# First block of a three-layer transformer: keys, values and indexer first as plain fp32, heads beside convolution projections, modulation in quarter slabs

## The chip, the cores and the metric

The kernel runs on one core of a Trainium2 chip. The core has TensorE (PE; weight loads are PEld), VectorE (DVE), ScalarE (ACT), GpSimd (POOL) and SyncE (SP), whose only work here is to issue DMAs in a queue of its own. The metric is device time in microseconds (us) of one execution, as a median of runs.

## The reference

One token mixer with a sparse indexer, modulated by a vector `c`, then a gated linear attention layer and a differential attention layer, all with feed-forwards, on 256 tokens of width 1024, batch 1, in fp32. The change lies in the first block:

```python
mod = c_act @ w_ada[l] + b_ada[l]                     # 1024 x 6144
sh1, sc1, g1, sh2, sc2, g2 = jnp.split(mod, 6, axis=-1)
mix = token_mixer(modulate(x, sh1, sc1), w_in[l], ...)
x = layer_norm(ALPHA * x + g1[:, None, :] * mix, ln1_g[l], ln1_b[l])
ff = swiglu(modulate(x, sh2, sc2), w_gate[l], w_up[l], w_down[l])
x = layer_norm(ALPHA * x + g2[:, None, :] * ff, ln2_g[l], ln2_b[l])
...
def token_mixer(h, w_in, conv_w, attn_norm_g, conv_norm_g, w_out, cos, sin):
    q, k, v, qi, ki, wi, gate_b, gate_c, hc = jnp.split(h @ w_in, offsets, axis=-1)
    # q (8 heads of 64), k (one head), qi (8 x 32) and ki get a partial rope
    # rel = relu(qi . ki); score = sum over heads of rel * wi; causal
    # each query keeps its 64 best keys; softmax attention of 8 heads over them
    attn = group_rms_norm(attn, attn_norm_g, N_HEADS_ATTN)
    u = gate_c * hc
    conv = sum(conv_w[j] * u_pad[:, j:j + s, :] for j in range(CONV_K))
    conv_out = group_rms_norm(gate_b * conv, conv_norm_g, CONV_GROUPS)
    return jnp.concatenate([attn, conv_out], axis=-1) @ w_out
```

## The kernel before

Activations lie transposed, features on the 128 partitions, as eight tiles of 128 x 256. Weights stream through two 2 MB buffers `raw` in SBUF (slots 0 and 1), 512 columns of a matrix at a time (a slab, 128 x 8 x 512). A product in near-fp32 is three fp32r matmuls: ScalarE rounds a slab into `whi` (`split`, L811), VectorE takes the rest into `wlo` (`low`, L1165), each in quarters of 1024 columns, and TensorE adds hi·hi, lo·hi and hi·lo (L1739 to L1741). A tile of output is 8 x 3 matmuls of 256 columns. The table of `Phase` objects (`plan`) fixes the order of the slabs, their slots and who must have read a buffer before it may be loaded again.

SyncE walks that table and waits, in order, for each buffer's reader. All engines run straight-line code, so what stands first on an engine runs first, and who waits holds up everything behind it.

The first block: slabs 0 to 3 of `w_ada` (shift and scale) are multiplied by `c` on VectorE, eight chunks of 512 columns (`modulate`, L1216 to L1221), and summed over partitions by TensorE (`modulation`, L1846, four matmuls with one column). GpSimd makes the modulated input `om` (L620), ScalarE its rounded form `ohi` (L883), VectorE `olo` (L1246). Then come the slabs `in_q`, `in_idx` (indexer queries, keys in copies), `in_v` (values and indexer weights), `in_gc`, the index scores, `in_hc` with the short convolution, the top-k on VectorE (L1325 to L1335), `in_gb`, and then the loop over eight heads. A head is: scores (PE L1927), masked logits and maxima (DVE L1360, L1363), exponentials (ACT L950), division (DVE L1371, L1374), transposes (PE L1943), `prob_t` (ACT L962), values (PE L1953). The modulation slabs 4, 5, 6, 7 and 11 go over ScalarE (`scale_by_c`, L924: eight chunks times `c`) and GpSimd (`sum_slab`, L631 to L635: three halving sums), and GpSimd issues their loads itself; slabs 8, 9 and 10 go over VectorE inside the head loop. All twelve are done ahead of `out0`, the output projection (two slabs, eight tiles), beside which TensorE sums the means and squares of layer norm 0 (L1968, L1970) one tile behind the residual addition (DVE L1405). Behind it: layer norm, `gate_up0`, `down0`, and the two other layers.

## Time and profile before

| what | us |
|---|---|
| median of 3 runs | 1215.05 (1214.82 to 1218.31) |
| the profiled execution | 1212.0 |
| its span | 1210.2 |
| TensorE busy | 1095.4 |
| VectorE busy | 753.9 |
| ScalarE busy | 585.8 |
| GpSimd busy | 258.9 |

Matmuls overlap, so a busy TensorE is not one at its peak: what counts is the distance between the starts of two matmuls and the granted clock (1.00 is 2.4 GHz, 0.50 is 1.2 GHz). The slabs are moved at up to some 400 GB/s, with a mean of 160 over the span.

### The profile page before, as it was taken

To read this page: it belongs to the slowest core of one execution; us is meant where nothing else is said; L and a number is where in the kernel's file an instruction comes from. 1 tells how busy PE (TensorE), PEld (TensorE's weight loads), DVE (VectorE), ACT (ScalarE), POOL (GpSimd) and SP (SyncE) were. 2 spreads that over 40 slices of the span, in tenths; PEclk is the share of its full clock that TensorE was granted. 3 is DMA by queue.
4 is the path that set the end of the run, shared out by engine and by line. 5 is a ranking of instruction groups with operands and counts; after the bars stand their busy time and mean duration, and the time that the engine had idled before them with its cause. 6 is when DMAs were issued, how large, how long until landed. Compare 5 with 4: busy or idle time off the path is not lost.

```text
span 1210.2 us, 20957 instructions
## 1 busy us (share of the span) xinstructions
PE 1095.4 (91%) x8179; PEld 1011.6 (84%) x8179; DVE 753.9 (62%) x1164; ACT 585.8 (48%) x989; POOL 258.9 (21%) x253
## 2 busy tenths in 40 slices
PE   1899638989999998999999999998997899999998
PEld 1887524879999996888899999997885599999997
DVE  5747876656655446775665664566777676655554
ACT  0545334574554338551564444465555664544452
POOL 0434332003332002101133331022120023332001
PEclk9988855999999999998999999998999999999999
DMA  8754454426554625350265455573432045554650
GB/s 317 219 209 164 184 189 159 144 81 219 184 186 126 206 79 207 141 210 1 70 209 184 169 160 157 169 273 112 162 116 100 1 166 204 186 186 123 200 186 36
DMA packets 188325, 193.46 MB, mean 160 GB/s; under 512 B 13721, under 2 KB 150722, under 8 KB 188130
## 3 DMA queue, kind: packets, MB, share of 16 engines
q1 hardware_dynamic: 184016, 179.88, 44.2%
q0 software_dynamic: 2640, 10.49, 2.3%
q10 hardware_dynamic: 1602, 2.18, 0.5%
q8 instruction: 45, 0.74, 0.2%
q14 instruction: 22, 0.18, 0.0%
HBM read 191.48 MB, written 1.05 MB: 159 GB/s over the span
## 4 chain that ended last, share of the span: by engine, by line
PE 65%; DVE 18%; ACT 6%; DMA 5%; issue 4%; POOL 1%; ACTq 1%; POOLq 0%; SPq 0%; DVEq 0%
PE gemm L1739 19%; PE gemm L1740 19%; PE gemm L1741 19%; DVE wlo L1165 5%; DVE macc L1218 2%; ACT whi L811 2%; DMA raw<-in_w_in 2%; PE aux L2062 1%; POOL om L620 1%; DVE xlo L1187 1%; PE aux L1846 1%; ACT om L984 1%; DMA early<-in_w_ada 1%; DMA raw<-in_w_ada 1%; ACT ohi L982 1%
## 5 line engine op out<-in xcount | busy, mean ns | idle before, releaser
L1165 DVE TENSOR_TENSOR wlo<-raw,whi 128x1024 fp32r<-128x1024 f32 (+2 forms) x348 | 399.6, 1195 | 137.3 <-ACT whi L811 137.0
L1739 PE MATMUL gemm<-ohi,whi 128*128 128x256 f32 x1536 | 436.7, 284 | 18.4 <-DVE wlo L1165 8.4
L1741 PE MATMUL gemm<-ohi,wlo 128*128 128x256 f32 x1536 | 431.4, 281 | 0.0
L1740 PE MATMUL gemm<-olo,whi 128*128 128x256 f32 x1536 | 431.1, 281 | 0.0
L811 ACT ACTIVATE whi<-raw 128x1024 fp32r<-128x1024 f32 (+2 forms) x348 | 309.5, 955 | 75.4 <-PE gemm L1741 52.2
L1739 PEld LDWEIGHTS gemm<-ohi,whi 128*128 128x128 f32 x1536 | 291.5, 190 | 28.9 <-DVE wlo L1165 11.9
L1740 PEld LDWEIGHTS gemm<-olo,whi 128*128 128x128 f32 x1536 | 291.6, 190 | 0.2
L1741 PEld LDWEIGHTS gemm<-ohi,wlo 128*128 128x128 f32 x1536 | 291.2, 190 | 0.0
L1739 PE MATMUL gemm<-acthi,whi 128*128 128x256 f32 x528 | 147.7, 280 | 0.0
L1740 PE MATMUL gemm<-actlo,whi 128*128 128x256 f32 x528 | 147.4, 279 | 0.0
L1741 PE MATMUL gemm<-acthi,wlo 128*128 128x256 f32 x528 | 147.3, 279 | 0.0
L664 POOL TENSOR_TENSOR prod<-sg,ut 128x256 f32<-128x256 f32 x66 | 48.7, 739 | 311.2 <-DVE ut L1492 163.8
L1739 PEld LDWEIGHTS gemm<-acthi,whi 128*128 128x128 f32 x528 | 99.1, 188 | 0.2
L1740 PEld LDWEIGHTS gemm<-actlo,whi 128*128 128x128 f32 x528 | 99.1, 188 | 0.0
L1741 PEld LDWEIGHTS gemm<-acthi,wlo 128*128 128x128 f32 x528 | 99.0, 188 | 0.0
L1010 ACT ACTIVATE sg<-gt 128x256 f32<-128x256 f32 x66 | 27.6, 418 | 133.2 <-DVE gt L1492 89.4
L668 POOL TENSOR_TENSOR actlo<-prod,acthi 128x256 f32 (+1 forms) x63 | 74.5, 1183 | 0.0
L1740 PE MATMUL gemm<-xlo,whi 128*128 128x256 f32 x256 | 72.3, 282 | 0.0
L1740 PEld LDWEIGHTS gemm<-xlo,whi 128*128 128x128 f32 x256 | 49.0, 191 | 1.4 <-issue 1.4
L701 POOL TENSOR_TENSOR sq_sum<-sq_sum,dsq 128x256 f32<-128x256 f32 x28 | 21.0, 748 | 129.6 <-ACT dsq L830 129.6
L1492 DVE TENSOR_TENSOR ut<-gemm,rstd 128x256 f32<-128x256 f32 x44 | 18.4, 419 | 48.2 <-PE gemm L1741 48.2
L1739 PE MATMUL gemm<-dhi,whi 128*128 128x256 f32 x128 | 39.8, 311 | 4.7 <-DVE xlo L1187 4.6
(315 smaller groups left out, 1508.6 us busy)
## 6 DMA issues: line engine op xcount, KB each, us to landing
raw<-in_ffn_w_in SPq DMA_DIRECT2D x44, 1024.0 KB, 6.3
raw<-in_ffn_w_out SPq DMA_DIRECT2D x32, 704.0 KB, 5.7
raw<-in_gla_w_in SPq DMA_DIRECT2D x6, 2048.0 KB, 7.8
raw<-in_diff_w_in SPq DMA_DIRECT2D x6, 2048.0 KB, 7.7
raw<-in_w_gate SPq DMA_DIRECT2D x11, 1024.0 KB, 5.1
raw<-in_w_up SPq DMA_DIRECT2D x11, 1024.0 KB, 7.3
raw<-in_w_down SPq DMA_DIRECT2D x16, 704.0 KB, 5.0
raw<-in_w_ada SPq DMA_DIRECT2D x5, 2048.0 KB, 8.3
```

The costliest lines, as they stand in the source:

```text
L620: me.did(pool.tensor_scalar(tl(om, t), tl(res, t), mod[:, 8 + t:9 + t], mod[:, t:t + 1], ALU.mult, ALU.add), om_ready)
L664: pool.tensor_tensor(tl(prod, j), tl(sg, j), tl(ut, j), ALU.mult).then_inc(prod_done, 1)
L668: pool.tensor_tensor(tl(actlo, t - 1), tl(prod, 1 - j), tl(acthi, t - 1).bitcast(F32), ALU.subtract).then_inc(actlo_ready, 1)
L701: pool.tensor_tensor(sq_sum[:, :], sq_sum[:, :], src, ALU.add).then_inc(squares_summed if last else sq_added, 1)
L811: act.activation(whi[hslot][:, q * w:(q + 1) * w], raw[slot][:, q * w:(q + 1) * w], ACT.Copy).then_inc(hi_ready, 1)
L1010: act.activation(tl(sg, j), tl(gt, j), ACT.Silu).then_inc(silu_done, 1)
L1165: dve.tensor_tensor(wlo[hslot][:, q * w:(q + 1) * w], raw[slot][:, q * w:(q + 1) * w], whi[hslot][:, q * w:(q + 1) * w].bitcast(F32), ALU. ...
L1218: me.link(dve.scalar_tensor_tensor(acc, src[:, 512 * k:512 * (k + 1)], c_act[:, k:k + 1], acc, ALU.mult, ALU.add))
L1492: ins = dve.tensor_tensor(dst, bank[:, 0:T], rstd[:, 0:T], ALU.mult)
L1739: pe.matmul(dst, st_hi, mv_hi, start=start, stop=False)
L1740: pe.matmul(dst, st_hi, mv_lo, start=False, stop=False)
L1741: return pe.matmul(dst, st_lo, mv_hi, start=False, stop=stop_)
```

## The change

- `in_idx` and `in_v` are gone. Their columns are one slab `in_kv` of 424 columns without copies, and TensorE multiplies them as plain fp32 with `om` (four banks, 8 x 4 matmuls of 256 columns), ahead of `in_q`. Keys and indexer keys are rotated once and copied to the other partitions by ScalarE; values are transposed.
- The index scores stand between the tiles of `in_q`; the top-k follows on VectorE, beside `in_gc`.
- The head loop has one tile of `in_hc` (heads 0 to 3) or `in_gb` (heads 4 to 7) in each head, with their convolution and gating steps. `in_gb` is split at heads 0 and 1, `out0` at heads 4 and 5.
- `om` and `ohi` both come from ScalarE. For slabs 0 to 3 VectorE takes six chunks and TensorE the last two; SyncE no longer waits for the parameter rows.
- Slabs 4, 5 and 6 keep the way over ScalarE and GpSimd, but their loads are in SyncE's queue; slab 6 is scaled and summed behind the head loop. Slabs 7 to 11 come in quarters (two chunks, 0.5 MB, two small buffers) and are taken by VectorE (`modulate_part`): slab 7 early, 8 and 9 one quarter beside each tile of `out0`, 10 and 11 one beside each slab of `gate_up0`.
- The transposes of `p` move from the first block into `down0`.

```diff
-    ada = lambda i: Phase(f"ada{i}", 1, SLAB, 0, 1, by="pool" if i in POOL_SLABS else "dve",
-                          ahead=False, ring=i not in (2, 3), slot=0 if i in (0, 8, 9, 11) else 1)
+    ada = lambda i: Phase(f"ada{i}", 1, SLAB, 0, 1, by="pool" if i in POOL_SLABS else "mod", ahead=False,
+                          ring=i not in (2, 3), slot=0 if i == 0 else 1)
+    mixer = lambda name, slot: Phase(name, 1, SLAB, 4, 1, ahead=False, slot=slot)
     phases = [
         ada(0), ada(1), ada(2), ada(3),
-        Phase("in_q", 1, SLAB, 4, 1, slot=0), Phase("in_idx", 1, SLAB, 4, 7, slot=1),
-        Phase("in_v", 1, 8 * 72, 2, 2, slot=0), ada(4), Phase("in_gc", 1, SLAB, 4, 1, slot=0), ada(5),
-        Phase("in_hc", 1, SLAB, 4, 1, slot=0), ada(6), Phase("in_gb", 1, SLAB, 4, 1, ahead=False, slot=0), ada(7),
-        ada(8), ada(9), ada(10), ada(11),
-        Phase("out0", 2, SLAB, 4, 1, slot=1), *ffn(0),
+        Phase("in_kv", 1, 8 * KV, 0, 1, by="kv", ahead=False, slot=0), mixer("in_q", 1), mixer("in_gc", 0), ada(4),
+        mixer("in_hc", 0), ada(5), mixer("in_gb", 0), ada(6),
+        Phase("out0", 2, SLAB, 4, 1, slot=0), *ffn(0),
...
+            def load_part(n):
+                wait(sp, part_used, n - 1)
+                dst, src = ada_part(n)
+                sp.dma_start(dst, src).then_inc(part_in[n % 2], 16)
...
+            parts = lambda *ns: [lambda n=n: load_part(n) for n in ns]
+            behind = {("ada1", 0): [load_x], ("in_q", 0): [*parts(0, 1), load_const, *parts(2, 3)],
+                      ("ada6", 0): parts(4, 5), ("gate_up0", 0): parts(6, 7), ("gate_up0", 1): parts(8, 9, 10, 11),
+                      ("gate_up0", 2): parts(12, 13), **{("gate_up0", i): parts(10 + i) for i in range(4, 10)},
...
-                if ph.by == "pool":
...
-                    if i == 0:
-                        sp.wait_ge(params_in, 16 * (len(ROWS_A) + len(ROWS_B) + 4))
...
+            for buf, ready in ((om, om_ready), (ohi, ohi_ready)):
+                for t in range(KT):
+                    me.did(act.activation(tl(buf, t), tl(res, t), ACT.Identity, bias=mod[:, t:t + 1],
+                                          scale=mod[:, 8 + t:9 + t]), ready)
...
+            def beside_head(i):
+                if i in (0, 1):
+                    split_all("in_gb", "in_gc", range(2 * i, 2 * i + 2))
+                if i == 2:
+                    scale_by_c(5)
+                if i in (4, 5):
+                    split_all("out0", "in_hc", range(2 * i - 8, 2 * i - 6))
+                if i == 6:
+                    group_squares(0, attn_ready, 2)
+                if i == 7:
+                    group_root(0, G[0])
+                    group_squares(2, gated_ready, 2)
+            exponentials(0)
+            for i in range(NH):
...
+            group_squares(1, attn_ready, 4)
...
+            prep(order=(4, 5))
+            group_root(3, X[0])
+            prep(order=(6, 7))
+            group_root(1, X[1])
+            prep(order=(2, 3))
             scale_by_c(6)
-            gemm("in_gb")
-            group_root((2, 3), mixed, mix_sq, 1.0 / HD, 0, X[0:2])
...
+            def modulate_part(n):
+                i, part_ = PART_SLABS[n // PARTS], n % PARTS
+                acc = MOD_SUM[i][:, :]
+                dve.wait_ge(part_in[n % 2], 16 * (n // 2 + 1))
+                if part_ == 0:
+                    wait(dve, mod_done, sum_free(i))
+                for j in range(2):
+                    k = 2 * part_ + j
+                    w, c = part[n % 2][:, 512 * j:512 * (j + 1)], c_act[:, k:k + 1]
+                    if k == 0:
+                        me.link(dve.tensor_scalar(acc, w, c, None, ALU.mult))
+                    else:
+                        me.link(dve.scalar_tensor_tensor(acc, w, c, acc, ALU.mult, ALU.add),
+                                part_used if j else None)
...
-            me.did(dve.tensor_tensor(fold[:, 32:40], A("ln2_g", 0, 8), B("norm_mix_2", 0, 8), ALU.mult))
-            me.link(dve.tensor_tensor(fold[:, 40:48], A("ln2_b", 0, 8), B("norm_mix_2", 0, 8), ALU.mult))
-            for q in range(4):
-                low(PH["out0"], At(0), q)
-            me.again(mixed_ready)
-            prep(mix_make, order=(0, 1, 2, 3))
+            masked_maxima(0)
+            for i in range(NH):
+                probabilities(i)
+                if i + 1 < NH:
+                    masked_maxima(i + 1)
+                for q in {1: (0, 1), 2: (2, 3)}.get(i, ()):
+                    low(PH["in_gb"], At(0), q)
+                for q in {5: (0, 1), 6: (2, 3)}.get(i, ()):
+                    low(PH["out0"], At(0), q)
+                if i < 4:
+                    short_conv(i)
+                else:
+                    gated_conv(i - 4)
+                if i in (2, 4, 6):
+                    take_pair(i // 2 - 1)
+            me.again(attn_ready)
+            prep(mix_make, order=(0, 1), free=PH["in_gb"].tile0 + 4)
+            take_pair(3)
+            me.again(gated_ready)
+            prep(mix_make, order=(4, 5))
+            prep(mix_make, order=(6, 7))
+            me.again(attn_ready)
+            prep(mix_make, order=(2, 3))
+            dve.wait_ge(mod_done, 7)
...
-            add_to_residual("out0", 16)
+            add_to_residual("out0", 16, lambda at, t: modulate_part(PARTS + 4 * at.i + t))
...
+                def part_beside(at, t):
+                    if t == 3 and 1 <= at.i <= 2 * PARTS:
+                        modulate_part(3 * PARTS + at.i - 1)
...
-                pe.wait_ge(pool_summed if i in POOL_SLABS else dve_summed, ph.used0 + 1)
+                if i < 4:
+                    src = raw[PH[f"ada{i}"].slot] if i < 2 else early[i - 2]
+                    pe.wait_ge(landed[i] if i < 2 else early_in[i - 2][1], 16)
+                    for k in (KT - 2, KT - 1):
+                        for m in range(4):
+                            pe.matmul(X[3][:, 4 * i + m:4 * i + m + 1], src[:, 512 * k + P * m:512 * k + P * (m + 1)],
+                                      c_act[:, k:k + 1], start=k == KT - 2 and m == 0, stop=False, skip_group_check=True)
+                    pe.wait_ge(dve_summed, i + 1)
+                elif i in POOL_SLABS:
+                    pe.wait_ge(pool_summed, POOL_SLABS.index(i) + 1)
...
+            modulation(2)
             modulation(3)
-            keep_warm(G[2], 13, ones[:, :])
+            keep_warm(G[2], 4, ones[:, :])
+            ph = PH["in_kv"]
+            w = flat(ph.slot, KT, KV)
+            pe.wait_ge(landed[ph.slot], ph.landed[0])
+            for k in range(KT):
+                pe.wait_ge(om_ready, k + 1)
+                for bank, (c0, c1) in zip(G, (K_V, KI_WI, QI_A, QI_B)):
+                    if k == 0:
+                        banks.claim(bank, rope_src)
+                    ins = pe.matmul(bank[0:c1 - c0, 0:T], w[:, k, c0:c1], tl(om, k), start=k == 0, stop=k == KT - 1)
+                    if k == KT - 1:
+                        ins.then_inc(kv_done, 1)
...
-                    h = i - 2
-                    bank, pt = X[h // 2 % 2], tl(prob_t, h % 2, w=384)
-                    if h % 2 == 0:
-                        banks.claim(bank, mixed_ready)
-                    me.next(pt_ready)
-                    rows = slice(HD * (h % 2), HD * (h % 2) + HD)
-                    pe.matmul(bank[rows, 0:T], vtok[:, 0:HD], pt[:, 0:T], start=True, stop=False,
-                              skip_group_check=True)
-                    pe.matmul(bank[rows, P:T], vtok[:, 72:72 + HD], pt[:, T:T + P], start=False, stop=True,
-                              skip_group_check=True).then_inc(pv_done, 1)
+                if i < 4:
+                    projection("in_hc", i, dve_read)
+                else:
+                    projection("in_gb", i - 4, gated_ready)
+                turned(i)
+                if i:
+                    values(i - 1)
+                if i == 1:
...
+                    group_stats((0,), C("blk"), mix_sq, G[0:1])
+                if i == 7:
...
-            gemm("out0", dve_read, olo_from=8, order=(4, 5, 6, 7, 0, 1, 2, 3),
-                 after=lambda at, t: mean_sums([4 * at.i + t - 1]) if 4 * at.i + t else None)
+            banks.claim(X[3], mod_read)
+            def beside_out0(at, t):
+                m = 4 * at.i + t
+                if m:
+                    mean_sums([m - 1])
+                if m in (1, 4, 7):
+                    modulation({1: 6, 4: 8, 7: 9}[m])
+            keep_warm(X[2], 2)
```

SyncE's queue from the second projection on, before and after. `raw_49` and `raw_50` are slots 0 and 1, `part` the quarter buffers; the wait is for the last reader of the buffer. Before:

```order
14 L586 DMA raw_49<-in_w_in 128x8x512 [waits lo_ready] x3
15 L586 DMA raw_49<-in_w_ada 128x8x512 [waits lo_ready]
16 L586 DMA raw_49<-in_w_ada 128x8x512 [waits dve_summed]
17 L586 DMA raw_50<-in_w_ada 128x8x512 [waits pool_summed]
18 L586 DMA raw_50<-in_w_out 128x8x512 [waits dve_summed]
19 L586 DMA raw_49<-in_w_out 128x8x512 [waits pool_summed]
20 L586 DMA raw_50<-in_w_gate 128x8x256 [waits lo_ready]
```

After:

```order
17 L611 DMA raw_49<-in_w_in 128x8x512 [waits lo_ready]
18 L611 DMA raw_50<-in_w_ada 128x8x512 [waits pool_summed]
19 L611 DMA raw_49<-in_w_in 128x8x512 [waits lo_ready]
20 L611 DMA raw_50<-in_w_ada 128x8x512 [waits pool_summed]
21 L577 DMA part_86<-in_w_ada 128x2x512 [waits part_used]
22 L577 DMA part_87<-in_w_ada 128x2x512 [waits part_used]
23 L611 DMA raw_49<-in_w_out 128x8x512 [waits lo_ready]
24 L611 DMA raw_50<-in_w_out 128x8x512 [waits pool_summed]
25 L611 DMA raw_49<-in_w_gate 128x8x256 [waits lo_ready]
```

Both halves of `in_w_out` stood behind the last sums of the modulation before; now each stands behind a sum of GpSimd with ada6 and two quarters ahead of the first.

VectorE at the end of the head loop and the start of `out0` (`om` and `olo` are the operand, `wlo` the low parts of the next slab, `res` the residual tile). Before:

```order
192 L1347 SCALAR_TENSOR_TENSOR om<-mixed,cols_a,mix_sq 128x256 [waits sd_ready,mixed_ready]
193 L1347 SCALAR_TENSOR_TENSOR om<-mixed,cols_a,mix_sq 128x256
194 L1187 TENSOR_TENSOR olo<-om,ohi 128x256 [waits ohi_ready]
195 L1347 SCALAR_TENSOR_TENSOR om<-mixed,cols_a,mix_sq 128x256 [waits sd_ready]
196 L1187 TENSOR_TENSOR olo<-om,ohi 128x256 [waits ohi_ready]
197 L1347 SCALAR_TENSOR_TENSOR om<-mixed,cols_a,mix_sq 128x256
198 L1187 TENSOR_TENSOR olo<-om,ohi 128x256 [waits ohi_ready] x2
199 L1165 TENSOR_TENSOR wlo_54<-raw_49,whi_52 128x1024 [waits hi_ready] x2
200 L1405 SCALAR_TENSOR_TENSOR res<-gemm,mod,res 128x256 [waits tile_done]
```

After:

```order
177 L1248 TENSOR_TENSOR olo<-om,ohi 128x256 [waits ohi_ready] x2
178 L1474 TENSOR_TENSOR mod<-aux,cols_a 128x8 [waits mod_done]
179 L1476 TENSOR_TENSOR lam<-lam 128x1 [waits lam_exp,mod_read]
180 L1477 TENSOR_SCALAR lam<-lam 128x1 [waits dve_step]
181 L1478 TENSOR_SCALAR lam<-cols_b 128x1 [waits dve_step]
182 L1222 TENSOR_TENSOR wlo_54<-raw_50,whi_52 128x1024 [waits hi_ready] x2
183 L1488 SCALAR_TENSOR_TENSOR res<-gemm,mod,res 128x256 [waits tile_done]
184 L1296 TENSOR_SCALAR acc_a<-part_86,c_act 128x512 [waits mod_done,part_in0]
185 L1298 SCALAR_TENSOR_TENSOR acc_a<-part_86,c_act,acc_a 128x512 [waits dve_step]
```

The low parts still stand ahead of the first residual, and behind each residual there is now a quarter of `w_ada`.

ScalarE between the last operand and `out0`, after (`raw_50<-raw_50,c_act` is the scaling of slab 6, `whi_52<-raw_50` the split of `out0`'s second half in the same buffer):

```order
104 L852 ACTIVATE ohi<-om 128x256 [waits om_ready] x2
105 L931 ACTIVATE raw_50<-raw_50,c_act 128x512 [waits landed1]
106 L931 ACTIVATE raw_50<-raw_50,c_act 128x512 x7
107 L820 ACTIVATE whi_52<-raw_50 128x1024 [waits landed1,tile_done]
108 L820 ACTIVATE whi_52<-raw_50 128x1024
109 L899 ACTIVATE ln_sq<-res 128x256 [waits dve_read]
```

Before, no scaling stood there:

```order
115 L843 ACTIVATE ohi<-om 128x256 [waits om_ready] x4
116 L811 ACTIVATE whi_52<-raw_49 128x1024 [waits landed0,tile_done]
117 L811 ACTIVATE whi_52<-raw_49 128x1024
118 L892 ACTIVATE ln_sq<-res 128x256 [waits dve_read]
```

The scaling, and the sum and the load that follow from it, moved in between.

## Rows read from the trace of the kernel before

**Rows 1.** Stretches: length, busy us per engine, granted clock, DMA share, GB/s.

```profile
37.30:57.50 20.20, 16.38 (x124) 15.61 (x123) 15.09 (x17) 12.41 (x20) 12.28 (x9) 0.92 0.68 187
140.80:210.20 69.40, 41.14 (x142) 26.76 (x142) 45.22 (x85) 26.66 (x67) 17.90 (x7) 0.53 0.48 180
210.20:247.90 37.70, 35.19 (x235) 30.32 (x234) 21.60 (x37) 19.23 (x29) 0.00 (x0) 1.00 0.50 168
247.90:1210.20 962.30, 917.70 (x7120) 863.56 (x7118) 590.57 (x866) 486.62 (x807) 193.57 (x213) 0.99 0.45 149
```

**Rows 2.** Timeline, all engines, start: start, us, instruction, idle before, its releaser.

```profile
15.73 0.99 SPq L572 DMA_DIRECT2D early<-in_w_ada  x2
...
29.73 1.87 PE L1846 MATMUL aux<-ones,macc 128*128 128x1 f32 x8 [6.32 <-DVE macc L1221]
...
35.63 1.05 PE L1846 MATMUL aux<-ones,macc 128*128 128x1 f32 x8 [0.30 <-DVE macc L1221]
...
37.31 10.23 POOL L620 TENSOR_SCALAR om<-res,mod 128x256 f32<-128x256 f32 x8 [36.29 <-DVE mod L1238]
...
40.47 4.03 ACT L883 ACTIVATE ohi<-res,mod 128x256 fp32r<-128x256 f32 x8
```

**Rows 3.** GB/s in 40 slices of 1.5 us, from 0 to 60 us.

```profile
GB/s 0 68 276 403 400 403 399 407 404 247 23 149 385 414 390 385 386 389 399 412 393 406 411 403 385 427 428 385 337 228 177 238 215 31 0 0 0 0 0 0
```

**Rows 4.** Timeline of TensorE: two fp32r matmuls, then two steps of fp32 ones.

```profile
136.91 0.28 PE L1740 MATMUL gemm<-olo,whi 128*128 128x256 f32 x1
137.02 0.28 PE L1741 MATMUL gemm<-ohi,wlo 128*128 128x256 f32 x1
...
246.77 0.59 PE L1968 MATMUL aux<-res,ones 128*128 128x256 f32 x2
247.21 0.59 PE L1970 MATMUL aux<-ln_sq,ones 128*128 128x256 f32 x2
```

**Rows 5.** Timeline of VectorE: index scores, top-k's ends, one head.

```profile
96.93 4.84 DVE L1306 SCALAR_TENSOR_TENSOR score<-relu,vtok,score 128x128 f32<-128x128 f32 x14
...
126.59 0.56 DVE L1325 TENSOR_TENSOR kept<-score,const 128x384 f32<-128x384 f32 x1
...
138.74 0.56 DVE L1335 TENSOR_TENSOR allow<-allow,const 128x384 f32<-128x384 f32 x1
...
200.65 0.56 DVE L1360 SCALAR_TENSOR_TENSOR logit<-gemm,allow 128x384 f32<-128x384 f32 x1 [1.44 <-PE gemm L1943]
201.24 0.61 DVE L1363 TENSOR_REDUCE neg_max<-logit 128x1 f32<-128x128 f32 x2
...
201.96 0.55 DVE L1374 TENSOR_SCALAR logit<-logit,rsum 128x128 f32<-128x128 f32 x2
```

**Rows 6.** One modulation slab on ScalarE and GpSimd; loads of 2 MB with us to landing.

```profile
102.31 5.02 ACT L924 ACTIVATE raw<-raw,c_act 128x512 f32<-128x512 f32 x8 [1.32 <-DMA raw<-in_w_ada]
...
107.42 4.63 POOL L631 TENSOR_TENSOR raw<-raw 128x2048 f32<-128x2048 f32 x1 [12.99 <-ACT raw L924]
112.13 3.22 POOL L632 TENSOR_TENSOR raw<-raw 128x1024 f32<-128x1024 f32 x1
115.42 1.26 POOL L635 TENSOR_TENSOR macc<-raw 128x512 f32<-128x512 f32 x1
...
raw<-in_w_in SPq DMA_DIRECT2D x3, 2048.0 KB, 8.0
```

**Rows 7.** Timeline of VectorE in out0: low parts, first residual, mean of the norm.

```profile
220.46 2.36 DVE L1165 TENSOR_TENSOR wlo<-raw,whi 128x1024 fp32r<-128x1024 f32 x2 [0.53 <-ACT whi L811]
222.73 0.48 DVE L1405 SCALAR_TENSOR_TENSOR res<-gemm,mod,res 128x256 f32<-128x256 f32 x1
...
247.91 0.42 DVE L1419 TENSOR_SCALAR mean<-aux 128x256 f32<-128x256 f32 x1 [1.31 <-PE aux L1970]
```

**Rows 8.** Timeline of VectorE: six chunks alone, and six while GpSimd sums.

```profile
146.99 4.69 DVE L1218 SCALAR_TENSOR_TENSOR macc<-raw,c_act,macc 128x512 f32<-128x512 f32 x6
...
160.68 11.73 DVE L1218 SCALAR_TENSOR_TENSOR macc<-raw,c_act,macc 128x512 f32<-128x512 f32 x6
```

More of the change, by code:

```diff
@@ L1313, in short_conv @@
+            me.next(v_src, 2)
+            add_heads(range(0, 4))
+            for q in range(4):
+                low(PH["in_gc"], At(0), q)
+            add_heads(range(4, IH))
+            def short_conv(t):
+                wait(dve, tile_done, PH["in_hc"].tile0 + t + 1)
+                bank = G[t]
                 u = upad[:, (T + 2) * t:(T + 2) * (t + 1)]
```

671 lines of the change are left out of this document (368 added, 303 removed).

## The prediction

> **What bounds the kernel now.** I read the stretches first: one row for each stage of the first block, one for everything behind its first layer norm [rows 1]. Behind 247.9 us TensorE is busy 917.7 of 962.3 us at a granted clock of 0.99; the change hardly touches that. Ahead of it, 140.8 to 210.2 stands out: TensorE busy 41 of 69 us, at a clock of 0.53. There the eight heads run alone, each a relay TensorE, VectorE, ScalarE, with the modulation slabs of w_ada squeezed in. So the time is set by a chain, and I walk the chain from rows: the start [rows 2, 3], the matmul prices [rows 4], the VectorE prices [rows 5], a w_ada slab's way through ScalarE and GpSimd and the time of a load [rows 6], the last stage, out0 [rows 7], and VectorE beside GpSimd [rows 8]. The end point of the walk is the `mean` of layer norm 0, at 247.91 before [rows 7]; what the change does to it is passed on undiminished, since TensorE is the bound behind it.
>
> **The start.** Before, SyncE issues the early slabs at 15.73, when the last parameter row has landed, so the transfers pause (slices of 1.5 us at 247, 23 and 149 GB/s), and the modulation is ready at 37.3, when GpSimd starts `om` [rows 2, 3]. After, nothing waits there. Four slabs of 2.10 MB and x (1.05 MB) are 9.4 MB; at the 400 GB/s of the full slices from about 4 us on they end at 27.5. VectorE takes six of eight chunks of a slab (six took 4.69 us [rows 8], a first one is shorter: 4.4 instead of 6.0), TensorE the other two, and that is more work for TensorE: 12 one-column matmuls a slab instead of 4. Eight records (4 matmuls) took 1.05 us at one time and 1.87 at another [rows 2], so a slab costs 3.2 or 5.6 us. TensorE has slab 1, 16 transposes of x (3.7 at the slower pace, 0.23 a record) and slabs 2 and 3 in a row from about 17 on, when the parameter rows are in: the modulation is ready between 32.5 and 37.5; I take 34. `om` then comes from ScalarE at 0.50 us a tile (`ohi` there, 4.03 for eight) instead of GpSimd's 1.28 (10.23 for eight) [rows 2].
> The plain fp32 gemm is 32 matmuls. Two of the same width stand 0.44 us apart [rows 4], so 13.9 us; it starts at 34.7 and ends at 50 with a slow first part. Its slab is 1.7 MB more in the same queue (32 us), so it is not late. The Trainium skill, SBUF — State Buffer, Summary: rules for kernel authors, says to count on about 358 GB/s between HBM and SBUF; by that the 9.4 MB would take 2.8 us more and all the loads below some 2 us more, and the forecast would be 5 us later. The slices in [rows 3] show 400 and more, and decide.
>
> **From the keys to the head loop.** VectorE has the chain: eight `olo`, in_q's four low parts, the residual scale and two w_ada quarters (a quarter is two chunks of 0.79, 1.6 us [rows 8]) keep it until 53; rotations 3.3, two more quarters to 60; four heads of index scores (0.69 each: 4.84 for seven [rows 5]), in_gc's low parts 4.7 (2.36 for two [rows 7]), four heads more: 70. The top-k took 126.59 to 139.3, 12.7 us [rows 5]: 83. Query rotations and in_hc's low parts: 91. The head loop then starts at 91, where before it started at 145.4. TensorE has in_q, in_gc and small things in that time (2 x 11.2 us at 0.117 us a matmul [rows 4]) and is not the bound.
>
> **The head loop and its first wait.** A head costs VectorE 0.56 + 0.61 for the masked maxima and 0.55 for the probabilities [rows 5], and now also a convolution or gating step and low parts; TensorE a 2.8 us projection tile and about 2 us of small matmuls. I get 5 to 6 us a head, set by the three in turn. ScalarE stands for about 3 us at head 0, where in_gb's slab lands late. It scales slab 5 at head 2, which I place at 108. Now SyncE's queue matters (the two listings of it under the change): ada6 waits for GpSimd's second sum, then two quarters, and only then out0's first half. Scaling 5.0, sums 4.6 + 3.2 + 1.3 at most and 8.4 as the middle [rows 6]: ada6 is issued at 122. Then 2.10 + 1.05 + 2.10 MB in one queue: 7.4 for the first (2 MB took a median of 8.0 from issue to landing [rows 6], one of them 7.4) and 3.15 MB at 400 GB/s for the rest, 15.3 in all: 137. But ScalarE has `split_all("out0")` at heads 4 and 5, ahead of head 4's prob_t. It reaches that at 119, so it **stands for 18 us**, and TensorE behind it for about 16. From 137, heads 4 to 7 (two at the lower clock) end at 158, group roots and operands at 168; out0's first tile is done at 169, against 222.7 before [rows 7]: 54 us gained here.
>
> **The second wait.** ScalarE scales slab 6 only now (168 to 173), GpSimd sums it (181.4), and only then may SyncE reload that buffer with out0's second half: landed at 189. VectorE has that half's low parts ahead of residual 0 (the listings of VectorE there), and TensorE, after its second tile (172), needs residual 0 for the mean sums. Before, the same two low parts waited 0.5 us for ScalarE [rows 7]. After: splits and low parts to 192.5, residual 0 at 193: TensorE **idle for about 21 us**. Then six tiles, the first at some 5.2 us (nearly double of 2.8, at the lower clock), mean sums 0.87 each (two fp32 matmuls [rows 4]), three modulations at 1.07, and VectorE's quarters between: VectorE is level with TensorE here (eight quarters 12.6, eight low parts 9.3, eight residuals 3.8, from 193 on). Slab 9's last quarter lies behind residual 7, then its modulation and nine small fold operations (taken as 1.3 together): 4 us on the path. The `mean` comes at 226.5. From residual 0 that is 33.5 us; before, 25.2 [rows 7].
>
> **Later.** Modulations 10 and 11 after gate_up0 are 16 records, 2.1 us, and the transposes of p move into down0: 8 records more, 1.0 to 1.2 us [rows 2]; both are on TensorE and paid: 3.3. The quarters beside gate_up0 cost 1.6 us of VectorE in a slab of 11 us, in which it is busy about 7: covered. GpSimd's sums beside VectorE are not free: six chunk operations took 11.73 instead of 4.69 us while GpSimd summed [rows 6, 8]; here slab 5's sum falls in heads 2 to 4, in front of a wait that swallows it, and slab 6's in an idle stretch. So 0, and 7 as the upper bound.
>
> **Sum.** 247.9 - 226.5 = 21.4, less 3.3: 18.1. Of the profiled execution's 1212.0 (span 1210.2 and 1.8 around it) that leaves 1193.9; the three runs have a median of 1215.05, 3 above it: 1197.
>
> **The rivals.** *The first wait is hidden.* If heads run slower than I count, or slab 5's sum ends early, out0's first half is there in time; the stretch to out0 shortens by up to 16. The second wait stays, since its order is written out. That gives 1181; with half of the second gone too, 1170. For it: I may have put ScalarE's arrival at head 4 too early. Against: the sum, the three loads and 15 us are fixed by rows.
> *The start stays at the lower clock.* At 1.2 GHz the fp32 gemm takes 27.8 instead of 13.9, and everything behind follows: 1211. Before, the stretch with in_q's first tiles had a granted clock of 0.92 over 20.2 us [rows 1], which is 3 us at the lower of two levels and so 1 to 2 us lost; that speaks against 14.
> *Slower than before: the clock doesn't come back.* Two long idle stretches and a head loop of short pieces leave TensorE at 1.2 GHz until layer norm 0, as it was in nearly all of 140.8 to 210.2 [rows 1]. Eight tiles in the head loop and six in out0 at 5.2 instead of 2.8 are 33, mean sums 6 more: 39, so 1236. It turns into a loss from 18 of these 39 on. Against it: in out0 before, the clock was 1.00 within a few us of dense tiles [rows 1]. The Trainium skill, TensorE: Matmul & The Clock Gate, Why this matters for your kernels, warns of just such gaps between bursts, after which the array is back at its lower clock; by that rule the four tiles behind the two waits run slow, which the walk has, and not all fourteen.
> *It doesn't do what it says.* Keys first, but the index scores still wait for something late (the rotation constants, which land at 43 by the queue's bytes, or the copies that spread the keys), and the loop starts no earlier. Against: each has 5 us of slack. It would give 1215.
>
> **Chances.** Forecast 0.60, first wait hidden 0.16, slow start 0.12, slower 0.07, no effect 0.05. A difference under 0.3% (3.6 us) can't be told from none. The slow start straddles that bound at its end: faster 0.86, same 0.07, slower 0.07. The range, 1176 to 1213, leaves out the slower case and the deep end of the hidden one; the forecast's own is 1185 to 1208, from the modulation's 5 us, GpSimd's 7 and the heads' pace.
>
> **What would show it.** The fp32 gemm over at 50, kept/top-k from 70, first `logit` at 91; ScalarE's whi waiting for raw<-in_w_out for 10 to 20 us in the middle of the heads, and again 15 to 20 us after out0's first tiles, with wlo behind it on VectorE and the mean sums idle on TensorE; `mean` at 226. If the two waits for in_w_out are absent, my reading of the queue is wrong; if they are there and the end is not, the pace of the stages is.

## The result

The changed kernel has a median of 1202.44 us (1200.84 to 1206.72, 4 runs) against 1215.46 (1214.82 to 1218.31, 4 runs) for the one before: a ratio of 0.9895, 95% interval 0.987 to 0.992. It is 13 us faster, where 18 were forecast. The profiled execution took 1200.84 us with a span of 1199.1, so 11.1 us of span came off.

The stretches of the changed kernel, columns as in [rows 1]: start, fp32 product, scores, top-k, heads until the first wait ends, last heads, operands, second wait, rest of out0, and all behind the `mean` of layer norm 0.

```profile
0.00:34.90 34.90, 24.30 (x124) 23.77 (x125) 17.63 (x28) 6.52 (x10) 0.48 (x7) 0.91 0.96 353
34.90:51.80 16.90, 16.90 (x66) 9.58 (x65) 12.40 (x20) 11.55 (x22) 0.57 (x1) 0.98 0.61 234
51.80:72.30 20.50, 16.21 (x105) 12.71 (x105) 16.78 (x31) 10.51 (x21) 3.52 (x4) 0.86 0.73 262
72.30:97.20 24.90, 19.10 (x146) 17.63 (x145) 24.35 (x59) 10.85 (x19) 9.77 (x4) 0.91 0.39 144
97.20:144.10 46.90, 35.98 (x207) 30.05 (x207) 30.95 (x63) 16.21 (x40) 8.23 (x3) 0.79 0.45 163
144.10:162.00 17.90, 15.46 (x80) 12.60 (x81) 8.58 (x18) 9.40 (x20) 0.00 (x0) 0.69 0.00 0
162.00:174.00 12.00, 4.99 (x15) 1.95 (x15) 7.23 (x21) 9.03 (x19) 0.00 (x0) 0.78 0.01 2
174.00:197.60 23.60, 9.88 (x52) 7.61 (x52) 2.42 (x4) 6.03 (x9) 8.22 (x3) 0.64 0.43 152
197.60:230.50 32.90, 30.99 (x201) 29.35 (x202) 22.62 (x40) 9.04 (x14) 0.00 (x0) 0.86 0.76 248
230.50:1199.10 968.60, 925.76 (x7144) 872.03 (x7142) 605.57 (x888) 486.52 (x807) 193.67 (x214) 0.98 0.46 153
```

The `mean` comes at 230.56 instead of 247.91 [rows 7]: 17.35 us won ahead of it, 6.2 lost behind it (968.5 instead of 962.3). The heads start 48 us earlier (97.2 for 145.4), but of the 100 us from there to 197.6 TensorE is busy only 66, and most of the other 34 us is two waits (TensorE stood idle for 7.8 us in the first and 19.6 in the second). They stand in ScalarE's timeline, in brackets the idle time before the row and its releaser:

```profile
115.19 5.00 ACT L931 ACTIVATE raw<-raw,c_act 128x512 f32<-128x512 f32 x8
...
144.10 2.00 ACT L820 ACTIVATE whi<-raw 128x1024 fp32r<-128x1024 f32 x2 [12.24 <-DMA raw<-in_w_out]
...
173.04 4.99 ACT L931 ACTIVATE raw<-raw,c_act 128x512 f32<-128x512 f32 x8
194.29 2.00 ACT L820 ACTIVATE whi<-raw 128x1024 fp32r<-128x1024 f32 x2 [16.26 <-DMA raw<-in_w_out]
```

The cause of both stands in SyncE's queue. The load of slab 6 goes out at 128.68, when GpSimd has summed slab 5, and only behind it out0's first half (the row at 130.23 holds both halves, 56.65 us from one to the other):

```profile
128.68 0.37 SPq L611 DMA_DIRECT2D raw<-in_w_ada  x1
129.09 1.09 SPq L577 DMA_DIRECT2D part<-in_w_ada  x2
130.23 56.65 SPq L611 DMA_DIRECT2D raw<-in_w_out  x2
```

A third loss I had set to zero: steps of VectorE that take long beside a sum of GpSimd. The rows of both engines, at the end of the top-k and in head 3; the second DVE row took 0.56 us before [rows 5]:

```profile
82.18 4.63 POOL L653 TENSOR_TENSOR raw<-raw 128x2048 f32<-128x2048 f32 x1 [3.62 <-ACT raw L931]
86.89 2.39 POOL L654 TENSOR_TENSOR raw<-raw 128x1024 f32<-128x1024 f32 x1
...
120.27 4.55 POOL L653 TENSOR_TENSOR raw<-raw 128x2048 f32<-128x2048 f32 x1 [29.43 <-ACT raw L931]
```

```profile
83.29 3.75 DVE L1400 TENSOR_SCALAR allow<-kept 128x384 f32<-128x384 f32 x1
87.07 2.63 DVE L1401 TENSOR_TENSOR allow<-allow,const 128x384 f32<-128x384 f32 x1
...
97.24 0.55 DVE L1428 SCALAR_TENSOR_TENSOR logit<-aux,allow 128x384 f32<-128x384 f32 x1
...
120.89 4.08 DVE L1385 TENSOR_SCALAR conv<-upad,cols_a 128x256 f32<-128x256 f32 x1
125.00 3.94 DVE L1387 SCALAR_TENSOR_TENSOR conv<-upad,cols_a,conv 128x256 f32<-128x256 f32 x2
```

Each long row ends within 0.5 us of the end of a GpSimd row beside it (87.04 and 86.81, 89.70 and 89.28, 124.97 and 124.82). Head 3's two rows took 0.35 and 1.01 in head 2. The Trainium skill, SBUF — State Buffer, Who interferes with whom, says that a GpSimd instruction that reads SBUF and a VectorE one that takes two inputs from SBUF, or runs in a two-port mode, shut each other out for the whole instruction. By that rule VectorE waits for an instruction's end and does not merely get slower; the trace agrees.

### The profile page after: what moved, and what is told of

The parts are those of the page before. It is cut to its first block, busy times and chain, and to the rows that moved or that the text cites. A ratio compares the mean times of both kernels' runs of the same rounds, so it can differ in the third digit from the quotient of the medians.

```text
span 1199.1 us, 20759 instructions
## 1 busy us (share of the span) xinstructions
PE 1099.6 (92%) x8133; PEld 1017.3 (85%) x8133; DVE 748.5 (62%) x1165; ACT 575.7 (48%) x977; POOL 224.5 (19%) x235
## 3 DMA queue, kind: packets, MB, share of 16 engines
HBM read 190.83 MB, written 1.05 MB: 160 GB/s over the span
## 4 chain that ended last, share of the span: by engine, by line
PE 68%; DVE 14%; ACT 7%; DMA 5%; issue 3%; POOL 2%; SPq 1%; POOLq 0%; DVEq 0%; ACTq 0%
PE gemm L1847 20%; PE gemm L1849 19%; PE gemm L1848 19%; DVE wlo L1222 4%; ACT whi L820 2%; DMA raw<-in_w_out 2%; PE gemm L1999 1%; DMA early<-in_w_ada 1%; PE aux L2252 1%; DMA raw<-in_w_in 1%; ACT raw L931 1%; POOL raw L653 1%; DMA raw<-in_gla_w_in 1%; PE aux L1962 1%; DVE xlo L1248 1%
## 5 line engine op out<-in xcount | busy, mean ns | idle before, releaser
L1222 DVE TENSOR_TENSOR wlo<-raw,whi 128x1024 fp32r<-128x1024 f32 (+2 forms) x340 | 386.7, 1185 | 135.5 <-ACT whi L820 134.9
L1848 PE MATMUL gemm<-olo,whi 128*128 128x256 f32 x1504 | 426.2, 283 | 0.0
L1849 PE MATMUL gemm<-ohi,wlo 128*128 128x256 f32 x1504 | 426.0, 283 | 0.0
L820 ACT ACTIVATE whi<-raw 128x1024 fp32r<-128x1024 f32 (+2 forms) x340 | 303.7, 961 | 95.9 <-PE gemm L1849 54.8
L677 POOL TENSOR_TENSOR prod<-sg,ut 128x256 f32<-128x256 f32 x66 | 51.2, 777 | 308.0 <-DVE ut L1585 163.8
L1067 ACT ACTIVATE sg<-gt 128x256 f32<-128x256 f32 x66 | 27.6, 418 | 133.5 <-DVE gt L1585 89.4
L681 POOL TENSOR_TENSOR actlo<-prod,acthi 128x256 f32 (+1 forms) x63 | 71.2, 1130 | 0.0
```

The source lines that it names most:

```text
L677: pool.tensor_tensor(tl(prod, j), tl(sg, j), tl(ut, j), ALU.mult).then_inc(prod_done, 1)
L681: pool.tensor_tensor(tl(actlo, t - 1), tl(prod, 1 - j), tl(acthi, t - 1).bitcast(F32), ALU.subtract).then_inc(actlo_ready, 1)
L820: act.activation(whi[hslot][:, q * w:(q + 1) * w], raw[slot][:, q * w:(q + 1) * w], ACT.Copy).then_inc(hi_ready, 1)
L1067: act.activation(tl(sg, j), tl(gt, j), ACT.Silu).then_inc(silu_done, 1)
L1222: dve.tensor_tensor(wlo[hslot][:, q * w:(q + 1) * w], raw[slot][:, q * w:(q + 1) * w], whi[hslot][:, q * w:(q + 1) * w].bitcast(F32), ALU. ...
L1848: pe.matmul(dst, st_hi, mv_lo, start=False, stop=False)
```

## The experiments

All are edits of the changed kernel (1202.4, ratio 0.9895 to the kernel before) unless a base is named. The kernel before had medians of 1216.2, 1214.1 and 1216.9 beside them; ratios are to it.

**The first wait.** SyncE's order, nothing else:

```diff
+                if ph.name == "ada6":
+                    held.append(load)
+                elif ph.name == "out0":
+                    load(At(0))
+                    held.pop()(At(0))
+                    load(At(1))
```

> Edit: SyncE issues the first half of w_out ahead of slab 6 and its two quarters, the rest is as in the changed kernel. Theory (the first wait is a queue position: 12.2 us of ScalarE in the middle of the heads, because that load stands behind GpSimd's second sum): it is issued when in_gb's low parts are done, about 117, and lands at about 126, before ScalarE gets to head 4 at 132. The row with 12.24 us idle for raw<-in_w_out goes, operands are ready at about 163 instead of 173.5, mean of layer norm 0 at about 220.5 instead of 230.6, median about 1192.5. The second wait stays, 16 us on ScalarE. Rival (the wait only swallows slack that the relay of the heads has anyway): the wait goes, but VectorE and TensorE take the same time for heads 4 to 7, and less than 3 us come off: 1199.5 or more.

Measured 1186.94 (0.9765, 0.974 to 0.9789). The first half goes out at 116.82, ScalarE splits it without a wait, the mean comes at 218.72 (11.8 earlier), and the second wait is as it was:

```profile
116.82 0.37 SPq L612 DMA_DIRECT2D raw<-in_w_out  x1
```

```profile
132.02 1.99 ACT L827 ACTIVATE whi<-raw 128x1024 fp32r<-128x1024 f32 x2
...
182.73 2.00 ACT L827 ACTIVATE whi<-raw 128x1024 fp32r<-128x1024 f32 x2 [16.20 <-DMA raw<-in_w_out]
```

So the wait was a place in a queue and cost its full 12 us (11.8 at the mean, 13.2 of the span, 15.5 in the medians, where 10 were expected); the relay of the heads had no slack to swallow it.

**The second wait.** Slab 6 scaled inside the first:

```diff
+                if i == 4:
+                    scale_by_c(6)
...
             prep(order=(2, 3))
-            scale_by_c(6)
```

> Edit: ScalarE scales slab 6 at head 4, where it stands for 12.2 us anyway, instead of behind the last operand. Theory (the second wait is one chain: scaling, sum, load): scaling hides in the stand (139 to 144), GpSimd sums until about 153, the second half of w_out lands at about 163, so neither ScalarE nor TensorE waits for it behind out0's first tiles. TensorE's 14.4 us of idle time in front of the first mean sums goes; mean at about 218, median about 1190. GpSimd's sum lies beside the low parts and mixing steps of heads 4 to 6 on VectorE and may give 2 to 4 us back. Rival (something else is late behind it, such as VectorE's low parts and quarters): residual 0 moves less than 5 us and the median stays above 1197.

Measured 1185.24 (0.9751, 0.9734 to 0.9769). No wait for w_out is left in out0: residual 0 at 178.25 instead of 197.66, mean at 210.62.

```profile
178.25 0.48 DVE L1489 SCALAR_TENSOR_TENSOR res<-gemm,mod,res 128x256 f32<-128x256 f32 x1 [4.45 <-PE gemm L1850]
```

This second wait is worth about 17 us: 17.2 in the medians, and 17.7 at the mean once the 2.2 are taken off by which this profiled run had its first logit earlier (95.05). That is 5 more than I expected, though GpSimd's sum stretched two low parts of `wlo` to 5.14 us.

**Both gone at the root.** Slab 6 in quarters on VectorE (SyncE's list moves by four quarters with it):

```diff
-POOL_SLABS = (4, 5, 6)
-PART_SLABS = (7, 8, 9, 10, 11)
+POOL_SLABS = (4, 5)
+PART_SLABS = (7, 6, 8, 9, 10, 11)
...
+                for q in dict(((0, (0, 1)), (4, (2,)), (5, (3,)))).get(i, ()):
+                    modulate_part(PARTS + q)
```

> Edit: slab 6 comes in quarters through VectorE as slabs 7 to 11 do (two quarters in head 0, one each in heads 4 and 5), so nothing is scaled or summed behind the heads, ada6 leaves the queue, and both halves of w_out are issued as soon as in_gb's low parts and slab 5's sum are done (about 117 and 129). Theory (both waits come from that slab alone): no row of 10 us or more idle for raw<-in_w_out is left; heads over at about 152 as with the first half moved up; residual 0 at about 172 instead of 197.7, mean at about 205, median about 1175. VectorE pays 6 us for the quarters, most of them in its idle time of heads 0, 4 and 5. Rival (VectorE becomes the bound of the heads): heads are 5 us longer, median 1180 or more.

Measured 1173.77 (0.967, 0.9649 to 0.9691): residual 0 at 169.54, mean at 200.48, no wait for w_out anywhere. It is 29 us off the changed kernel, what the two single edits gave together (15.5 and 17) less 4.

```profile
169.54 0.48 DVE L1490 SCALAR_TENSOR_TENSOR res<-gemm,mod,res 128x256 f32<-128x256 f32 x1 [3.43 <-PE gemm L1851]
```

**Slabs on TensorE.** No scaling, no sums (the loop is the core of the edit):

```diff
+                    for k in range(KT):
+                        for m in range(4):
+                            ins = pe.matmul(X[3][:, 4 * i + m:4 * i + m + 1],
+                                            raw[ph.slot][:, 512 * k + P * m:512 * k + P * (m + 1)], c_act[:, k:k + 1],
+                                            start=k == 0 and m == 0, stop=k == KT - 1, skip_group_check=True)
```

> Edit: slabs 4, 5 and 6 are multiplied by c on TensorE (32 matmuls with one column each, slab as stationary operand), no scaling on ScalarE, no sums on GpSimd; slab 4 behind slab 7's modulation, 5 at head 1, 6 at head 4. Theory (GpSimd's sums set both waits, and block VectorE beside them: 4.7 us at the end of the top-k, about 7 in head 3): first logit at 92.5 instead of 97.2, no operation of VectorE in head 3 over 1.2 us, first wait at most 5 us, second wait gone; the 96 matmuls cost TensorE 13 to 22 us, of which some 5 lie on the path. Mean at about 203, median 1172 to 1178. Rival (the heads are bound by TensorE at its lower clock, where these matmuls land): the waits go, but 10 to 15 us come back in the heads, median 1186 or more.

Measured 1194.33 (0.9834, 0.9804 to 0.9864): the rival. The waits and the blocked steps are gone (`allow` 0.36 and 0.56), but the 96 matmuls took 34 us, not 13 to 22 (10.97, 13.81 and 9.29, at a granted clock of 0.64, 0.50 and 0.77), and VectorE waited 33.8 us for TensorE behind them:

```profile
89.62 10.97 PE L1957 MATMUL aux<-c_act,raw 128*128 128x1 f32 x64
...
118.15 13.81 PE L1957 MATMUL aux<-c_act,raw 128*128 128x1 f32 x64
```

```profile
102.28 0.56 DVE L1431 SCALAR_TENSOR_TENSOR logit<-aux,allow 128x384 f32<-128x384 f32 x1 [10.29 <-PE aux L2087]
```

Here 32 matmuls are 64 records. [rows 2] would have said it: eight records, four matmuls, took 1.05 or 1.87, so 32 take 8.4 or 15; I had taken a record for a matmul.

**What a sum blocks.** Three runs. First the sums in seven instructions of 512 columns:

```diff
-                me.link(pool.tensor_tensor(w[:, 0:2048], w[:, 0:2048], w[:, 2048:4096], ALU.add))
-                me.link(pool.tensor_tensor(w[:, 0:1024], w[:, 0:1024], w[:, 1024:2048], ALU.add))
+                for k in range(2, KT):
+                    me.link(pool.tensor_tensor(w[:, 0:512], w[:, 0:512], w[:, 512 * k:512 * (k + 1)], ALU.add))
```

> Edit: GpSimd sums a slab in seven additions of 512 columns instead of 2048, 1024 and 512 columns; the same number of sums. Theory (VectorE's operation with its operands in SBUF waits until the running GpSimd instruction ends, whatever its own length): the long rows of VectorE get shorter, from 3.75 and 2.63 at the top-k's end and 4.08 in head 3 to at most 1.2 above their own time (2.3, 1.8 and 1.6), and GpSimd's pieces wait for VectorE in turn; the first logit comes 2 to 3 us earlier, the whole 2 to 5 us: about 1199. Rival (the two engines share a rate): cutting the sums changes nothing, VectorE's time beside a slab's sum stays as long in all, first logit at 97 and 1202.

```profile
86.88 0.63 DVE L1400 TENSOR_SCALAR allow<-kept 128x384 f32<-128x384 f32 x1
87.54 1.53 DVE L1401 TENSOR_TENSOR allow<-allow,const 128x384 f32<-128x384 f32 x1
...
92.41 6.76 DVE L1222 TENSOR_TENSOR wlo<-raw,whi 128x1024 fp32r<-128x1024 f32 x4
...
123.76 0.48 DVE L1385 TENSOR_SCALAR conv<-upad,cols_a 128x256 f32<-128x256 f32 x1
124.27 2.87 DVE L1387 SCALAR_TENSOR_TENSOR conv<-upad,cols_a,conv 128x256 f32<-128x256 f32 x2
```

The rows behave as blocking by instructions wants (2.2 instead of 6.4 us, 3.4 instead of 8.0), which a shared rate would not do. The time does not follow: 1206.7 (0.991, 0.9884 to 0.9936), not to be told from the changed kernel. The seven pieces take longer than the three sums: slab 4's 11.2 us instead of 8.7, which now reach into in_hc's low parts (6.76 us, in the changed kernel 4.62), so half of the 4.2 us won at the top-k is lost again. The top-k also began 3.6 us late in this profiled run (see the last section), the first logit came at 99.10, and slab 5's sum, begun 2.5 us later and 1.3 longer, ended at 132.5 instead of 128.7, which lengthened the first wait to 17.25 us. Second, slab 4's sum beside the top-k's rounds:

```diff
             relus(range(4, IH))
+            scale_by_c(4)
             for t in (2, 3):
                 take("in_q", t, tl(rope_in, t), rope_src)
-            scale_by_c(4)
...
+            sum_slab(4)
             query_cosines(8, 2, "cos_q")
```

> Edit: only slab 4 moves: ScalarE scales it before it takes in_q's last two tiles, and GpSimd sums it before the last query rotation, so the sum lies beside the rounds of the top-k (max and match_replace, one input in SBUF) and not beside its last two steps. Theory (a GpSimd sum stops only VectorE's steps with two SBUF inputs, or a tensor_scalar from SBUF to SBUF; the max and match rounds run on): scaling 71 to 76, sum 76 to 85, the rounds keep their 11.0 us, the last two steps take at most 2.5 instead of 6.4 us, first logit at about 93.5 instead of 97.2, median about 1198.5. Rival (anything of VectorE is slowed beside GpSimd): the rounds get longer by what the last steps lose, first logit stays at 97, median 1202.

Measured 1198.94 (0.9876, 0.9856 to 0.9897), first logit at 94.32.

```profile
77.91 4.61 POOL L653 TENSOR_TENSOR raw<-raw 128x2048 f32<-128x2048 f32 x1 [7.96 <-ACT raw L932]
```

```profile
84.77 0.43 DVE L1401 TENSOR_SCALAR allow<-kept 128x384 f32<-128x384 f32 x1
85.24 1.52 DVE L1402 TENSOR_TENSOR allow<-allow,const 128x384 f32<-128x384 f32 x1
```

The sum ran beside the rounds of max and match_replace, which took 11.0 us (73.76 to 84.77) as in the changed kernel, where the sum begins only at 82.18 (72.28 to 83.29). So those rounds are not blocked. The kernel before shows it too: a sum of GpSimd lay beside them from 130.06 on, and they took 11.0 us (126.59 to 137.60). The first logit came 2.9 us earlier and the mean 3.3; the median is 3.5 us lower, though the intervals overlap. Third, with slab 5's as well, below.

**A kernel that beats both.** On the quarters of slab 6: slab 4's sum early and two small loads of layer 1 one place later, then slab 5 scaled at head 3.

```diff
-                      ("gla_z", 0): [load_gates]}
+                      ("gla_q", 0): [load_gates]}
```

> Edit: slab 6 in quarters (as in the run before), slab 4's sum beside the top-k's rounds, and the two small loads of the gating weights of layer 1 one place later in SyncE's queue, behind the next slab. Theory: the gains add up: 3.7 us from slab 4, 1.3 us from the loads (the row whi idle 3.75 us for raw<-in_gla_w_in back to the 2.45 of before); median about 1170. Rival (the first logit's gain is swallowed by the load of in_gb's slab, for which ScalarE already waits 2.6 us in head 0): 1173 or more.

Measured 1171.84 (0.9634, 0.9601 to 0.9667), 2 us below its base where 5 were expected, and the intervals overlap. In the profile slab 4's gain is there at the first logit (94.75 instead of 97.37) and gone at the mean (200.85 and 200.48): the granted clock was 0.66 where out0 begins (160 to 170) and 0.84 at its end (190 to 201), in the base 0.82 (163 to 172) and 0.97. The loads gave nothing: from the mean of layer norm 1 to the gating product it takes 27.6 us, in the changed kernel 27.3, before 26.0. That guess of mine fell.

```diff
-                if i == 2:
+                if i == 3:
                     scale_by_c(5)
...
-                if i == 5:
-                    modulation(5)
                 if i == 6:
+                    modulation(5)
                     modulation(6)
```

> Edit: as the run before, and slab 5 is scaled at head 3 instead of head 2, its modulation and slab 6's on TensorE in head 6; its sum then lies beside heads 4 and 5, whose mixing step reads PSUM, and not beside the convolution of head 3 (three steps on SBUF, 8.0 instead of 1.35 us). Theory (what the sum costs hangs on which VectorE step it meets): no step of head 3 over 1.1 us, the sum meets two probability steps and perhaps two low parts, 2 to 4 us in place of 6.7; median 3 to 4 us below the run before, about 1166. Rival: the same loss in another place, no difference.

Measured **1166.95** (0.9618, 0.958 to 0.9655): 47 us below the kernel before, 35 below the changed one. Against the run before it is 4.9 in the medians, with intervals that overlap; out0's low parts, behind the last operand, begin 3.8 us earlier (157.26 for 161.10). Head 3's steps are back at 0.35 and 1.01; the sum now meets a probability step and the low parts of out0 (3.9 us lost together, where head 3 lost 6.7):

```profile
118.67 0.35 DVE L1386 TENSOR_SCALAR conv<-upad,cols_a 128x256 f32<-128x256 f32 x1
119.06 1.01 DVE L1388 SCALAR_TENSOR_TENSOR conv<-upad,cols_a,conv 128x256 f32<-128x256 f32 x2
...
126.85 2.33 DVE L1442 TENSOR_SCALAR logit<-logit,rsum 128x128 f32<-128x128 f32 x2
...
130.21 4.51 DVE L1223 TENSOR_TENSOR wlo<-raw,whi 128x1024 fp32r<-128x1024 f32 x2
...
194.14 0.42 DVE L1515 TENSOR_SCALAR mean<-aux 128x256 f32<-128x256 f32 x1
```

**Parts of the change undone.** GpSimd makes `om` again:

```diff
...
+            for t in range(KT):
+                pool.tensor_scalar(tl(om, t), tl(res, t), mod[:, 8 + t:9 + t], mod[:, t:t + 1], ALU.mult,
+                                   ALU.add).then_inc(om_ready, 1)
...
```

> Edit: one part of the change undone: om comes from GpSimd again (1.28 us a tile), ScalarE makes only ohi. Theory (the speed of om does not matter once it runs ahead of the fp32 product): a step of that product takes 2.05 us, GpSimd's tile 1.28, so every tile of om is there in time; the product ends at most 1 us later than 51.7, first logit within 1 us of 97.2, median about 1203, not to be told from the changed kernel. Rival (the 6 us that ScalarE saves on om are on the path): 1208.

Measured 1201.36 (0.9879, 0.9843 to 0.9915): no difference, as expected. The eight tiles took 6.07 us, not the 10.23 of [rows 2]; there VectorE's low parts ran beside them for 4.83 us, here they came behind them.

```profile
36.03 6.07 POOL L661 TENSOR_SCALAR om<-res,mod 128x256 f32<-128x256 f32 x8 [35.01 <-DVE mod L1320]
```

The wait for the parameter rows, ahead of the early slabs:

```diff
+                    if i == 0:
+                        sp.wait_ge(params_in, 16 * (len(ROWS_A) + len(ROWS_B)))
```

> Edit: another part undone: SyncE waits again for the parameter rows before it issues the early slabs. Theory (the pause in the transfers at 14 to 18 us costs what it lasts): the first early load is issued at about 15 instead of 6.3, the modulation is ready 3 to 4 us later (37 instead of 33.5), first logit at about 100.5, median about 1206. Rival (VectorE's six chunks a slab set the pace, not the loads): modulation at 34, no difference.

Measured 1203.08 (0.9895, 0.9861 to 0.9929): the rival, no difference. The four loads are issued from 13.47 instead of 6.31, but the last of them at the same time, and the next slab at 16.87 instead of 16.84: with x and two slabs ahead of them, they are not missed. The modulation was ready at 35.5 instead of 33.0, but so it was in six variants without this wait (see the last section).

```profile
13.47 3.36 SPq L601 DMA_DIRECT2D early<-in_w_ada  x4
16.87 8.01 SPq L613 DMA_DIRECT2D raw<-in_w_in  x2
```

The projections of in_hc taken out of the heads:

```diff
             pe.wait_ge(roped, 4)
+            for t in range(4):
+                projection("in_hc", t, dve_read)
             scores(0)
...
-                if i < 4:
-                    projection("in_hc", i, dve_read)
-                else:
+                if i >= 4:
                     projection("in_gb", i - 4, gated_ready)
```

> Edit: the four tiles of in_hc's projection stand ahead of head 0's scores instead of one in each of heads 0 to 3. Theory (in heads 0 to 3 VectorE is the bound, so TensorE's tile is hidden there): the first logit comes 11 us later, at about 108.5, heads 0 to 3 get only 3 us shorter (the idle 3.2 us of head 0), median about 1209. Rival (heads 0 to 3 are bound by TensorE): they get shorter by what was moved, 1203.

Measured 1216.79 (1.0001, 0.9984 to 1.0018, 10 runs): these four tiles outside the heads cost 13 to 14 us and eat the whole gain of the change.

```profile
111.76 0.56 DVE L1428 SCALAR_TENSOR_TENSOR logit<-aux,allow 128x384 f32<-128x384 f32 x1 [14.23 <-PE aux L2073]
```

The seven steps from the first logit to the eighth take 52.6 us instead of 55.1. So in heads 0 to 3 TensorE's tile is hidden but for 2.5 us, as the theory had it; VectorE is the bound there (in the changed kernel it has no wait in its rows from 104.6 to 131.2). The tiles outside took 14.2 and not 11. This is the only large part of the change that was undone; what the fp32 product of the keys or the quarter slabs are worth alone no run shows.

## Why the prediction was right, and where its sum was off

The direction and the two waits with their cause were right, and both waits of ScalarE lie within the sizes named as signs (12.2 for 10 to 20, 16.3 for 15 to 20); the saving was 11.1 of span instead of 18.1. Step by step:

- *Start.* The modulation at 33.0 (forecast 34). The fp32 product ended at 51.7, not 50: 32 matmuls took 17.0 us. I had priced them at 0.44 each from the mean sums [rows 4], whose stationary operand is the same each time; here they stand 0.51 apart. This is no clock: in 36 to 48 us the granted clock was 1.00 and a step of four took 2.05; only the first step, at 2.51, lost 0.5 to the lower level. The rival "slow start" is out. Two explanations that I gave for gains here were worth nothing: the wait for the parameter rows and ScalarE's `om`, as the two undone parts show.
- *To the head loop.* in_gc's slab landed at 62.8, behind slab 7's quarters, and VectorE waited 2 us: top-k from 72.3 (70). First logit at 97.24 (91). The top-k took 17.4 us and not 12.7, and these 4.7 are the term that I set to zero, GpSimd's sum beside VectorE at the top-k's end. **This is the step that failed**: I looked for a wait that swallows the sums and found one for slabs 5 and 6, and did not ask what VectorE does beside slab 4's. Moving that sum brought the mean forward by 3.3. For slab 5 the walk was right: its 6.7 us in head 3 lie ahead of a wait whose end the load sets, so here they cost nothing. They cost time once the wait is gone: there, moving that sum gave some 4 to 5 us.
- *First wait.* ScalarE at head 4 at 131.9 (119), the half landed at 144.0 (137), 12.2 us of standing (18). Both ends are late, by 13 and by 7: the late first logit lies ahead of both, but the blocked head 3 only ahead of ScalarE's arrival, since slab 5 had been scaled before it. So the stand came out shorter and its end no earlier. Its cause is shown by the swap in the queue. The rival that it is hidden is out.
- *Second wait.* Scaled from 173.0 (168), landed at 194.3 (189), residual 0 at 197.66 (193). TensorE idle 5.2 and 14.4, 19.6 in all (21). From residual 0 to the mean 32.9 (33.5).

```profile
173.73 3.78 PE L1945 MATMUL aux<-const,ones 128*128 128x512 f32 x4 [5.23 <-DVE mod L1474]
...
198.28 1.19 PE L2130 MATMUL aux<-res,ones 128*128 128x256 f32 x2 [14.40 <-DVE res L1488]
```

- *Clock.* 0.79 and 0.69 in the heads, 0.64 in the second wait, 0.86 from 197.6. Before, 140.8 to 210.2 had 0.53 [rows 1]. It came back within the first tiles behind each wait, at 155 and 206 us, some 9 and 8 after TensorE's first matmul there, as the walk had it; the slower case is out.
- *Later.* 6.2 instead of 3.3, and 967.2 to 970.4 us behind the mean in the profiles of the eleven variants (968.5 in the changed kernel). By landmarks: gate_up0 1.4 (quarters on VectorE, which I called covered), its end to down0's first residual 1.8 (modulations 10 and 11; forecast 2.1), the next tile 0.9 (transposes of p; 1.0 to 1.2), layer norm 1 to the gating product 1.3, the rest 0.9. The 1.3 is one load of in_gla_w_in, issued 12.7 us behind that mean in both kernels and landed in 9.0 us instead of 7.7 (ScalarE waits 3.75 us for it instead of 2.45). Why it took longer stays open; the two small loads were not it.

So 4.1 us of the 7.0 that are missing lie ahead of the mean (6 us late at the first logit, 7 where out0's first half lands, 5 at the last operand, 4 at the mean), 2.9 behind it. The quarters beside gate_up0, which I called covered, are 1.4 of these.

## What to carry to other kernels

A load's place in a queue is worth what stands in front of it: follow every moved step to the buffer that it frees and to the load behind that, and ask which reader comes first; here two placements cost 29 us. Beside a long GpSimd instruction, put VectorE steps such as max and match_replace, or those with an input in PSUM, which ran unchanged here (`logit` 0.54 us at 129.10 beside slab 5's sum in the fastest run), but no steps with two inputs in SBUF and no tensor_scalar from SBUF to SBUF; and take a price only from a row without such a neighbour. Undo single parts before you credit them: of three parts undone here, one took the whole gain with it and two took nothing.
